# Block-wise feed-forward products in a hybrid diffusion transformer: activations normalised ahead of the products, another order of the seven products, adaLN chunks spread over three feed-forward blocks

## What is computed

```python
def modulate(h, g, shift, scale):
    return rmsnorm(h, g) * (1 + scale) + shift

def adaln_terms(s, w, b):
    return jnp.split(jax.nn.silu(s) @ w + b, N_MOD, -1)

def swiglu(x, w_up, w_down):
    gate, up = jnp.split(x @ w_up, 2, -1)
    return (jax.nn.silu(gate) * up) @ w_down
...
h = h + 0.5 * ml[2] * swiglu(modulate(h, norm_g[i, 0], ml[0], ml[1]), ffn_w_up[i, 0], ffn_w_down[i, 0])
...
h = h + 0.5 * ml[8] * swiglu(modulate(h, norm_g[i, 2], ml[6], ml[7]), ffn_w_up[i, 1], ffn_w_down[i, 1])
```

## Time and profile before

| | |
|---|---|
| median of 3 runs | 3221.68 us (3221.12 to 3222.01) |
| the profiled execution | 3219.07 us |
| its span, first to last instruction | 3217.3 us |
| busy: PE, PEld | 2915.9 us (91%), 2686.9 us (84%) |
| busy: DVE, ACT, POOL | 2195.6 us (68%), 1246.8 us (39%), 1191.0 us (37%) |
| mean granted TensorE clock | 0.972 |

### The profile page before, as it was taken

How to read it: one execution, slowest core, us unless ns; L and a number is a source line. 1 busy time by engine, 2 the same in 40 slices (tenths; PEclk the granted TensorE clock), 3 DMA queues, 4 the chain that set the end, 5 groups by cost and what they waited for, 6 DMA issues and landing times.

```text
span 3217.3 us, 48134 instructions
## 1 busy us (share of the span) xinstructions
PE 2915.9 (91%) x18175; PEld 2686.9 (84%) x18175; DVE 2195.6 (68%) x3480; ACT 1246.8 (39%) x2501; POOL 1191.0 (37%) x909
## 2 busy tenths in 40 slices
PE   8788999899999988988888978999999989988998
PEld 8688888799988877978878878899998877877887
DVE  6887887786546665678888877565566457456666
ACT  5223332343454455323322234333333336533333
POOL 1634233223332213463324333533333234554443
PEclk9899999899999999999999999999999999999999
DMA  6333344223320032233324322112221210222222
GB/s 235 119 100 102 108 125 136 100 69 111 132 68 14 8 92 83 86 105 105 113 98 150 125 95 76 49 64 66 78 68 60 84 34 2 86 69 93 82 79 79
DMA packets 140227, 285.46 MB, mean 89 GB/s; under 512 B 41774, under 2 KB 63198, under 8 KB 139870
## 3 DMA queue, kind: packets, MB, share of 16 engines
q1 hardware_dynamic: 137262, 275.98, 26.5%
q10 hardware_dynamic: 2736, 6.40, 0.5%
HBM read 270.73 MB, written 15.10 MB: 89 GB/s over the span
## 4 chain that ended last, share of the span: by engine, by line
PE 51%; DVE 26%; issue 10%; ACT 8%; POOL 3%; DMA 2%; SPq 0%; ACTq 0%; POOLq 0%; DVEq 0%
PE psum L2254 28%; PE psum L2272 12%; DVE wl L1784 6%; DVE ada_product L1966 5%; DVE sq L1727 3%; DVE h L2215 2%; PE psum L2462 2%; ACT wh L1258 2%; POOL wl L1135 1%; DMA raw<-in_w 1%; PE psum L2545 1%; DVE o_acc L2086 1%; ACT sq L1282 1%; PE psum L2568 1%; POOL stats L1160 1%
## 5 line engine op out<-in xcount | busy, mean ns | idle before, releaser
L1135 POOL TENSOR_TENSOR wl<-raw,wh 128x512 fp32r<-128x512 f32 (+3 forms) x278 | 470.3, 1692 | 1026.8 <-ACT wh L1258 1022.4
L1258 ACT ACTIVATE wh<-raw 128x512 fp32r<-128x512 f32 (+2 forms) x713 | 458.5, 665 | 348.1 <-DMA raw<-in_w 246.0
L2254 PE MATMUL psum<-uh,wh 128*128 128x256 f32 (+5 forms) x1552 | 403.2, 341 | 49.8 <-DVE h L2215 32.2
L1784 DVE TENSOR_TENSOR wl<-raw,wh 128x512 fp32r<-128x512 f32 x432 | 339.3, 796 | 114.5 <-ACT wh L1258 114.2
L2254 PE MATMUL psum<-uh,wl 128*128 128x256 f32 (+5 forms) x1552 | 395.9, 337 | 0.0
L2254 PE MATMUL psum<-ul,wh 128*128 128x256 f32 (+5 forms) x1552 | 395.5, 336 | 0.0
L1966 DVE SCALAR_TENSOR_TENSOR ada_product<-ada_w,cb 128x1024 f32<-128x1024 f32 x256 | 390.7, 1526 | 4.7
L2254 PE MATMUL psum<-ah,wh 128*128 128x512 f32 (+4 forms) x1040 | 308.9, 360 | 61.2 <-DVE h L2215 29.2
L2215 DVE SCALAR_TENSOR_TENSOR h<-psum,mod,h 128x512 f32<-128x512 f32 x360 | 214.3, 632 | 205.7 <-PE psum L2254 205.2
L2254 PEld LDWEIGHTS psum<-uh,wh 128*128 128x128 f32 (+1 forms) x1552 | 258.0, 191 | 81.9 <-DVE h L2215 41.6
L2272 PE MATMUL psum<-ah,wh 128*128 128x386 f32 (+3 forms) x864 | 289.7, 335 | 15.5 <-ACT held L1276 15.5
(11 more groups left out here) (329 smaller groups left out, 5657.3 us busy)
## 6 DMA issues: line engine op xcount, KB each, us to landing
raw<-in_w SPq DMA_DIRECT2D x232, 512.0 KB, 3.8
ada_w<-in_ada_w SPq DMA_DIRECT2D x128, 512.0 KB, 3.7
raw<-in_w SPq DMA_DIRECT2D x160, 256.0 KB, 2.7
spill<-cacc ACTq DMA_DIRECT2D x16, 384.0 KB, 2.4
scale_w<-in_scale_w SPq DMA_DIRECT2D x8, 512.0 KB, 14.8
raw<-in_w SPq DMA_DIRECT2D x32, 128.0 KB, 2.0
ada_w<-bias_final SPq DMA_DIRECT2D x16, 256.0 KB, 3.1
ada_start<-in_ada_w SPq DMA_DIRECT2D x7, 512.0 KB, 16.0
```

Source lines behind the costliest of these rows:

```text
L1135: nc.gpsimd.tensor_tensor(weight_tile(x, wl), raw[raw_place[slot_of[x]][0]][:, 0:n], weight_tile(x, wh).bitcast(f32), ALU.subtract).then_i ...
L1258: nc.scalar.activation(weight_tile(x, wh), src, ACT.Copy).then_inc(hi_split, 1)
L1784: nc.vector.tensor_tensor(weight_tile(x, wl), pair_weight(x), weight_tile(x, wh).bitcast(f32), ALU.subtract).then_inc(pair_lo, 1)
L2254: ins = nc.tensor.matmul(pair[0:w, lo:hi], wt[:, k * w:(k + 1) * w], xt[:, k, cols], start=first, stop=last)
```

## The change

- **Order of the products** in a chunk: P6 P7 P5 P1' P4 P3 P2' becomes P6 P7 P1' P5 P2' P4 P3 (the dash marks the next chunk).
- **The add onto P7**: ScalarE copies P7 into `af` (`hold_product`), and VectorE adds u4 onto that (`up_halves`); P2 is read by `gate_first`.
- **Normalised ahead**: the tiles for the pair products now hold `h` times scale times `rstd`. VectorE makes them (`t_make`), in eight steps per block: four in part 0 for the sums, four more beside part 0's downs, where all of `uh`/`ul` is written anew (`u_highs`, `u_lows`). The multiplications by `rstd` in the pair part fall away; Silu is done in pieces, one straight from the bank of P3, and the gating per half. P1 waits for all eight low splits.
- **Part 0's downs** go in the order 0, 4, 1, 5, 2, 6, 3, 7.
- **adaLN chunks**: 48, 40 and 40 in blocks (0,0), (0,1) and (1,0), in place of 56, 72 and 0; none stands beside part 0's downs.
- **Columns**: context first, the two shift columns side by side at 256 and 257, latent tokens behind; the shift columns of all eight tiles are written by one instruction per engine.

```diff
@@ -39,9 +39,10 @@
 SUMS = {"P7": 1, "P6": 2, "P5": 3, "P3": 4}
 LATE_NORMS = (0, 1, 2, 3, 4, 5)
 TU = T + 2
-AT = 512 - TU // 2 + 1
-U_CTX, U_LAT = 1, 1 + T_CTX
+U_CTX, SHIFT, U_LAT = 0, T_CTX, T_CTX + 2
 WIDE, NARROW = TU // 2 + 1, TU // 2 - 1
+AT = 512 - NARROW
+FIRST_DOWNS = (0, 4, 1, 5, 2, 6, 3, 7)
...
@@ -60,10 +61,9 @@
                 continue
             if j == CLASSIC:
                 items += [("P1",) + key, ("P2",) + key]
-            items += [("P6",) + key, ("P7",) + key, ("P5",) + key]
             after = [(kind,) + chunks[j + 1] for kind in ("P1", "P2")] if j + 1 < FFC else []
-            items += after[:1] + [("P4",) + key, ("P3",) + key] + after[1:]
-        items += [("down", layer, f, part, i) for i in range(KD)]
+            items += [("P6",) + key, ("P7",) + key] + after[:1] + [("P5",) + key] + after[1:] + [("P4",) + key, ("P3",) + key]
+        items += [("down", layer, f, part, i) for i in (range(KD) if part else FIRST_DOWNS)]
     return items
...
@@ -86,16 +86,24 @@
     def shares(x):
         if x[0] == "down":
-            return 1 if x[3] < 2 else 2
-        return {"gate": 2, "up": 2, "P7": 1, "P1": 1, "P2": 1}.get(x[0], 0)
+            return 2
+        return {"gate": 1, "up": 1, "P7": 1, "P1": 1, "P2": 1}.get(x[0], 0)
     kinds = ("gate", "up", "down") + PAIR
-    at = [i for i, x in enumerate(items) if x[0] in kinds and x[1:3] == (0, 0)][FUSED:]
-    n = next(k for k, i in enumerate(at) if items[i][0] == "down")
-    over(at[:n], ada_chunks(0, [2]))
-    over([i for i in at[n:-2] for _ in range(shares(items[i]))], ada_chunks(0, range(3, N_MOD)))
-    at = [i for i, x in enumerate(items) if x[0] in kinds and x[1:3] == (0, 1)][:-2]
-    over([i for i in at for _ in range(shares(items[i]))], ada_chunks(1, range(N_MOD)))
+    def ahead_of_downs(layer, f):
+        at = [i for i, x in enumerate(items) if x[0] in kinds and x[1:3] == (layer, f)]
+        return at[:next(k for k, i in enumerate(at) if items[i][0] == "down")]
+    def later_parts(layer, f):
+        at = [i for i, x in enumerate(items) if x[0] in kinds and x[1:3] == (layer, f) and x[3]]
+        return [i for i in at[:-2] for _ in range(shares(items[i]))]
+    over(ahead_of_downs(0, 0)[FUSED:], ada_chunks(0, [2]))
+    over(later_parts(0, 0), ada_chunks(0, range(3, 8)))
+    over(ahead_of_downs(0, 1), ada_chunks(0, [8]))
+    over(later_parts(0, 1), ada_chunks(1, range(4)))
+    over(later_parts(1, 0), ada_chunks(1, range(4, N_MOD)))
     return plan
...
@@ -509,9 +519,10 @@
                 return [(start_gain, KD)]
             if kind in PAIR:
                 q = pair_no[x[1:]]
...
+                if x in held_no:
+                    return [(held_copied, held_no[x] + 1)]
+                return [{"P2": (quarter_added, 3 * q + 1), "P4": (quarter_added, 3 * q + 3),
+                         "P3": (silu_done, silu_no[("second",) + x[1:]] + 1)}.get(kind)]
             if kind in RESIDUAL:
...
@@ -855,23 +877,25 @@
             ahead = [j for j, y in enumerate(l2_items) if number[y] == at + 4]
...
+                    T_MAKE.update({at("up", 1): 0, at("gate", 2): 1, at("gate", 3): 2, at("up", 3): 3})
+                    T_HIGHS.update({at("up", 2): 0, at("gate", 3): 1, at("up", 3): 2, downs[0]: 3})
+                    T_LOWS.update({at("gate", 3): 0, at("up", 3): 1, downs[0]: 2, downs[1]: 3})
                 else:
...
+                    T_MAKE.update({at("up", 0): 0, at("gate", 1): 1, at("gate", 2): 2, at("up", 2): 3})
+                    T_HIGHS.update({at("up", 1): 0, at("gate", 2): 1, at("gate", 3): 2, at("up", 3): 3})
+                    T_LOWS.update({at("gate", 2): 0, at("up", 2): 1, at("up", 3): 2, downs[0]: 3})
...
+                ub, vb = (t[:, halves(x)[1]] for t in uv[j % 2])
+                pool.wait_ge(t_made, KD * ffn_no(x) + HALF_K + j + 1)
+                nc.gpsimd.tensor_tensor(ub, vb, ub, ALU.subtract).then_inc(t_added, 1)
             def norm_heads(u):
...
@@ -1265,22 +1282,32 @@
             def hold_product(x):
...
                 if x[0] == "P1":
...
+                    act.wait_ge(t_low, KD * ffn_no(x) + KD)
+                q, cols = pair_no[x[1:]], columns_of(x)
                 act.wait_ge(product_done, number[x] + 1)
...
+                if x[0] == "P7":
+                    act.wait_ge(a_lo, glu_no[x[1:]])
+                    kept = af[:, from_first(x, cols)]
+                else:
+                    kept = {"P1": t1, "P6": u2, "P5": u4}[x[0]][:, 0:width_of(cols)]
+                    if q:
+                        act.wait_ge(quarter_added, 3 * q - 3 + {"P1": 1, "P5": 2, "P6": 3}[x[0]])
+                nc.scalar.activation(kept, bank_cols(x, cols), ACT.Copy).then_inc(held_copied, 1)
+            def silu_first(x):
+                act.wait_ge(quarter_added, 3 * pair_no[x[1:]] + 1)
+                for t, b in half_pieces(x, sg, 0):
                     ins = nc.scalar.activation(t, t, ACT.Silu, bias=b)
                 ins.then_inc(silu_done, 1)
+            def silu_second(x):
+                act.wait_ge(product_done, number[x] + 1)
+                act.wait_ge(glu_done, glu_no[x[1:]])
+                (t, b), = half_pieces(x, sg, 1)
+                nc.scalar.activation(t, bank_cols(x, columns_of(x)), ACT.Silu, bias=b).then_inc(silu_done, 1)
...
+            def u_highs(x, j):
+                act.wait_ge(t_added, 5 * HALF_K * ffn_no(x) + 4 * HALF_K + j + 1)
                 act.wait_ge(product_done, number[("down",) + x[1:3] + (0, 0)])
...
+                cols = slice(halves(x)[0].start, TU)
+                for t, k in zip(uv[j % 2], (j, HALF_K + j)):
+                    ins = nc.scalar.activation(u_of(x)[0][:, k, cols], t[:, cols], ACT.Copy)
+                ins.then_inc(t_high, 1)
             def square(m, i):
...
+            def gate_first(x):
+                q, first = pair_no[x[1:]], halves(x)[0]
+                wide_ = width_of(first)
+                dve.wait_ge(product_done, number[("P2",) + x[1:]] + 1)
+                dve.wait_ge(held_copied, held_no[("P1",) + x[1:]] + 1)
+                dve.wait_ge(glu_done, glu_no[x[1:]])
+                nc.vector.tensor_tensor(sg[:, 0:wide_], t1[:, 0:wide_], bank_cols(("P2",) + x[1:], first), ALU.add) \
+                    .then_inc(quarter_added, 1)
+            def up_halves(x):
+                q, (first, second) = pair_no[x[1:]], halves(x)
                 head, tail = from_first(x, first), from_first(x, second)
...
+                dve.wait_ge(held_copied, held_no[("P5",) + x[1:]] + 1)
+                nc.vector.tensor_tensor(af[:, tail], u4[:, 0:width_of(second)], af[:, tail], ALU.add).then_inc(quarter_added, 1)
+                dve.wait_ge(product_done, number[x] + 1)
+                dve.wait_ge(a_lo, glu_no[x[1:]])
+                nc.vector.tensor_tensor(af[:, head], u2[:, 0:width_of(first)], bank_cols(x, first), ALU.add).then_inc(quarter_added, 1)
+                dve.wait_ge(quarter_added, 3 * q + 3)
+                dve.wait_ge(silu_done, silu_no[("first",) + x[1:]] + 1)
+                gated_half(x, 0)
+            def gated_half(x, half):
+                for (t, b), (gate, _) in zip(half_pieces(x, af, half), half_pieces(x, sg, half)):
+                    ins = nc.vector.scalar_tensor_tensor(out=t, in0=t, scalar=b, in1=gate, op0=ALU.add, op1=ALU.mult)
+                return ins
+            def gated_second(x):
+                dve.wait_ge(silu_done, silu_no[("second",) + x[1:]] + 1)
+                gated_half(x, 1).then_inc(glu_done, 1)
...
@@ -1793,12 +1791,30 @@
                     ins = nc.vector.tensor_tensor(low, src, high.bitcast(f32), ALU.subtract)
                 ins.then_inc(t_low, 1)
...
+            def t_make(x, s):
+                m = norm_of(x)
+                if m:
+                    dve.wait_ge(mod_ready, mod_terms(("norm", m), 0, 1))
+                if s >= 2:
+                    dve.wait_ge(t_low, KD * ffn_no(x) + s - 1)
+                term, j = mod[:, m // 3, :, :, :], s % HALF_K
+                shift, scale = 3 * (m % 3), 3 * (m % 3) + 1
+                for t, k in zip(uv[j % 2], (j, HALF_K + j)):
+                    for v, (lo, hi) in enumerate(segs_of(x)):
+                        cols = u_cols(lo, hi)
+                        nc.vector.scalar_tensor_tensor(out=t[:, cols], in0=h[:, k, lo:hi], scalar=term[:, scale, k, v:v + 1],
+                                                       in1=rstd[:, cols], op0=ALU.mult, op1=ALU.mult)
+                    ins = nc.vector.tensor_copy(t[:, SHIFT:U_LAT], term[:, shift, k, :])
+                ins.then_inc(t_made, 1)
+            def u_lows(x, j):
+                (high, low), cols = u_of(x), slice(halves(x)[0].start, TU)
                 dve.wait_ge(t_high, KD * ffn_no(x) + HALF_K + j + 1)
...
+                for t, k in zip(uv[j % 2], (j, HALF_K + j)):
+                    ins = nc.vector.tensor_tensor(low[:, k, cols], t[:, cols], high[:, k, cols].bitcast(f32), ALU.subtract)
+                ins.then_inc(t_low, 1)
...
```

(19 more changed lines are left out.)

211 lines of the change are left out of this document (59 added, 152 removed).

## The result

The changed kernel takes 3182.77 us (median of 4 runs, 3176.74 to 3185.49), the kernel before 3221.4 in the same comparison: a ratio of 0.9879 (95% interval 0.9862 to 0.9896). It is faster by 38.6 us, 1.2%, where 116 were forecast. The time lies inside the stated range (3050 to 3185), by two us, but the gain is a third of the forecast.

The account below looks back on a forecast made before the run. TensorE's idle time, largely waits for bank 3's release, was taken as the bound, counted 1.4 times. -103 (full blocks), -33 (last block) and +20 (part 0) on 3219.1 gave 3103, plus 2.6 for the median: 3105; range 3050 to 3185.

Parts of the forecast that it names:

- What bounds the kernel: Feed-forward blocks: TensorE's idle time, largely waits for L1755, which empties bank 3, counts about 1.4 times.
- The full blocks, -103 forecast: Parts 1 to 5 of (0,0), (0,1), (1,0): 453, 451 and 453 us in place of 498, 528 and 434.
- Block (1,1), -33 forecast: Last block, latent tokens only: 19.1 us of waits and half of 8.8 saved, 23.5 times 1.4.
- four fifths of the L1755 and L1276 waits as gone: Bank 3 addition and copy waits: (0,0) saves 28.7 of 35.9 us, (0,1) 45.3 of 56.6, (1,1) 19.1 of 23.9.
- The part on the adaLN chunks: Parts 1 to 5: moved chunks shift TensorE's update waits, (0,1) 17.7 to 10, (1,0) 1.4 to 12.5; SyncE's added loads cost nothing.
- Rival B: Behind P3, late gating holds ScalarE's copy of P6 and hi splits: slower, +176 us, 3281; chance 0.06.
- Rival A: Load, not order: TensorE's time follows VectorE's busy time; blocks 472, 456, 480, total 3174; chance 0.13.
- 36 us over 18 chunks: Pair products: VectorE's work falls by three scalings, 2.25 us per chunk, less about 0.2 for gating in pieces.
- VectorE near 365 of (1,0): Sign that the forecast is right: VectorE's busy time in parts 1 to 5 of block (1,0), in us.
- rival D: Nothing left to wait for: the kept fifth of waits and part 0's 20 don't come, -54 us, 3051; chance 0.06.
- Part 0, +20 forecast: Sum tiles made by VectorE, eight times per block: +9, +3, +5, +3 us; range -5 to +40.
- Rival C: Shared port in part 0: each wide half of a making waits 0.5 us more, +42 us, 3147; chance 0.07.

Follow-up runs that it names:

- experiment 4: Changed kernel with the old order of products (P6 P7 P5 P1' P4 P3 P2') taken back, all else of the change kept: 3052.98 us, ratio 0.9473.
- experiment 5: Kernel before with only the change's adaLN plan (48, 40, 40 in place of 56, 72, 0): 3220.08 us, ratio 0.9996.
- experiment 10: As experiment 4, but VectorE adds u4 onto P7 straight from bank 3, at P5, and ScalarE copies no P7: 3093.21 us, ratio 0.9596.
- experiment 7: As experiment 4, but VectorE adds u4 onto P7 from bank 3, one product late in its queue; no ScalarE copy of P7: 3159.08 us.
- experiment 6: As experiment 4, but with the adaLN plan of the kernel before (56, 72, 0): 3071.3 us, ratio 0.9539.
- experiment 9: As experiment 4, but the last four of eight makings per block, beside part 0's downs, leave out their multiplications: 3043.1 us, ratio 0.9439.

## Why the prediction came out wrong

**What bounds the kernel** was read rightly as far as it went: the waits for L1755 were there to be removed, and idle time of TensorE counts about 1.4 times. From the changed kernel to experiment 4, (1,1) loses 42.9 us of idle time and 58.1 of length: 1.35.

**The full blocks, -103 forecast: -82 measured** (-33.9, -72.9, +24.8 for -45, -77, +19). VectorE in (1,0) is busy 354 us (365 said), TensorE 430 to 432 in each (425 to 435). The waits for bank 3 are 1.4 us, none and 0.3. But idle time is 32.3, 23.4 and 29.0 where 20.8, 18.9 and 20.8 were said; ten of it in each is the new wait for the last low half ahead of the downs. Waits for residual updates came out lower than said, 7.4 in (0,1) and 8.7 in (1,0) for 10 and 12.5.

**Block (1,1), -33 forecast: +23.5 measured.** This is the step that failed: "four fifths of the L1755 and L1276 waits as gone" for every block. 56 of the 74 us by which the sum was off lie here. L1755's waits did go, with 7.4 us left for bank 3's other release; the copies' waits were to shrink since "P6 to P5 has two products between in place of one", and went from 8.4 us to 29.1 here, and from 28.4 to 54.9 over the four blocks. The wait for `al` ahead of the downs was to halve from 8.8 and rose to 20.6.

**The cause was in a step costed at nothing.** The part on the adaLN chunks looked at SyncE's queue and at the DMA share (0.19), said "so I cost this at nothing", and asked only what the added loads displace. It didn't ask when a weight buffer comes free. The order of products sets that: it moves P3 one place later and P1' one place earlier, and takes two of five products from the load. The DMA engines were idle most of the time (share 0.23 in (1,1)), and the load was late all the same, because it started late; with two more buffers (1,1) takes 307.3 us in place of 361.5. I had counted what the new order gives to each bank and had not counted what it takes from each buffer. Rival B had the place right (ScalarE in order, P5 behind the copy of P6, late gating) and the trigger wrong: it blamed work of VectorE in the full blocks and priced 176 us there; it was loads, and it struck where products are shortest. Rival A, *load, not order*, at 3174 is nearest to the measured time, and by chance: its (0,1) and (1,0) were to be 456 and 480 and came out at 455 and 459, and (1,1) has the other sign.

**What each part is worth** comes out of the chain of kernels. Plan alone: -1 (experiment 5). From there to experiment 10, which adds the normalising ahead with its lighter VectorE, the Silu and gating in pieces and the column layout: -127. ScalarE's copy of P7: -40. The new order: +130. The -127 are 149 us less in parts 1 to 5 and 23 more in part 0. The forecast gave the gain to copy and order; most of it lies in this step. The lighter VectorE, which I had entered as "36 us over 18 chunks" and then used only for rival A and for the sign "VectorE near 365 of (1,0)", is the likely reason: VectorE's busy time in parts 1 to 5 falls by 38 us in each full block, for 44, 36 and 42 us of length (experiment 5 to 10). But it was not tried by itself. That a single low half ahead of the addition is worth 66 us (experiment 7 against 10) speaks for what stands ahead of L1755 as much as for its one product of slack; which of the things in the -127 did how much of it was not taken apart. The chain has one order; with the parts removed in another, the shares would differ (experiment 6 shows the plan worth 18 in place of 1).

**Without the new order the mechanism would have given more than forecast**: 436, 433 and 437 in the full blocks, under the 453, 451 and 453; that is near what rival D, nothing left to wait for, had priced for the changed kernel (3051, and experiment 4 took 3053).

**Part 0, +20 forecast: +16 measured** (7.7, 3.9, 2.7, 1.7 for 9, 3, 5, 3). The terms are right within 2.3 us each, in part by luck: the plan alone takes 3.0 and 5.3 us off (0,0) and (0,1) (experiment 5), and the split between first and second makings was wrong (experiment 9). The first update of (0,0) starts 5.7 us later, at 136.4, where some 9 were said. Rival C, whose price was the shared port (its own figures give 40 us, not 42), is not borne out as a term: the wide halves of the makings took 0.75 into `stats` and 0.90 into `held`, not well over 1. Its mechanism is there, but seldom: 46 of the 64 ran beside no GpSimd instruction, at 0.75 each, and the other 18 took 1.02 on average.

```profile
L1806 DVE SCALAR_TENSOR_TENSOR held<-h,mod,rstd 128x512 f32<-128x512 f32 x32 | 28.6, 895 | 0.7
...
L1806 DVE SCALAR_TENSOR_TENSOR stats<-h,mod,rstd 128x512 f32<-128x512 f32 x32 | 23.8, 747 | 0.7
```

## What to carry to other kernels

When products, chunks or steps change places, count for every ring of buffers how many steps lie between the release of a buffer and its first new use, and compare that time, in the stage with the shortest steps, with a load's duration. A low DMA share (0.23 here) says nothing about it: a load that starts late is late on an idle queue. A wait for a load inside an engine that works in order costs whatever others await behind it, so read what the awaited engine itself waited for, before putting the wait down to its work. And when an addition or a copy is to be undone for a comparison, it has to go back to its exact place in the queue: one place was worth more here than the copy.

## What the runs showed of the hardware

VectorE's low halves take longer when GpSimd works beside them. In (1,1) of the changed kernel VectorE makes two low halves at 2954.55, of which one alone takes 0.69, in 3.46 us, while GpSimd sums weights:

```profile
2954.55 3.46 DVE L1782 TENSOR_TENSOR wl<-raw,wh 128x512 fp32r<-128x512 f32 x2
```
```profile
2954.42 1.35 POOL L1130 TENSOR_TENSOR held<-raw 128x512 f32<-128x512 f32 x1
2955.85 1.60 POOL L1141 TENSOR_TENSOR raw<-raw 128x512 f32<-128x512 f32 x1
```

The two low halves together take the two sums' time and a little more (2.95 us and 0.5), as if each waited for one of them. The Trainium skill, SBUF — State Buffer, section Who interferes with whom, says that a VectorE instruction with two SBUF inputs and a GpSimd instruction that reads SBUF exclude each other; these rows agree. So do all the low halves of pair weights (L1782) in the changed kernel: the 395 that no GpSimd instruction overlapped took 0.69 us on average and none more than 0.70, the 109 that one overlapped took 1.33 on average and up to 1.78. The late loads are not what brings the two together: in experiment 4, without them, 160 are overlapped, at 1.19 on average. What this costs the kernel in all, no run here separates.
